# Relative bias of the attention scores: an identity matmul on TensorE in place of an addition on VectorE

## The reference

```python
def diff_attention(q, k, v, rel_bias, lam):
    for i in range(S // Q_BLOCK):
        q0 = i * Q_BLOCK
        end = q0 + Q_BLOCK
        s = jnp.einsum('bqhmd,bkhmd->bhmqk', q[:, q0:end], k[:, :end]).astype(jnp.float32) * scale
        rel = jnp.arange(q0, end)[:, None] - jnp.arange(end)[None, :]
        bias = jnp.transpose(bias_tab[t5_bucket(rel)], (2, 0, 1))
        s = s + bias[None, :, None]
        s = jnp.where(rel >= 0, s, -jnp.inf)
        p = jax.nn.softmax(s, axis=-1)
        a = p[:, :, 0] - lam * p[:, :, 1]
        outs.append(jnp.einsum('bhqk,bkhv->bqhv', a.astype(v.dtype), v[:, :end]))
```

## Time and profile before

| | |
|---|---|
| median of three executions | 2799.29 us |
| profiled execution, its own time | 2801.21 us |
| its span in the trace | 2799.4 us |
| TensorE busy | 2624.7 us, 94% |
| VectorE busy | 1155.1 us, 41% |
| ScalarE busy | 831.7 us, 30% |
| mean granted TensorE clock | 0.969 |

### The profile page before, as it was taken

How to read it: one execution, slowest core, us unless ns; L and a number is a source line. 1 busy time by engine, 2 the same in 40 slices (tenths; PEclk the granted TensorE clock), 3 DMA queues, 4 the chain that set the end, 5 groups by cost and what they waited for, 6 DMA issues and landing times. The chain is left out here.

```text
span 2799.4 us, 30661 instructions
## 1 busy us (share of the span) xinstructions
PE 2624.7 (94%) x12450; PEld 2124.2 (76%) x12450; DVE 1155.1 (41%) x1839; ACT 831.7 (30%) x1463; POOL 140.8 (5%) x165
## 2 busy tenths in 40 slices
PE   8699989879999999999999998996999999999997
PEld 7588866658788888878777886764878888887876
DVE  0556355645333321135662455555531111113554
ACT  0422244434211111134553124444421111113343
POOL 0001100002000000001010010000200000000000
PEclk9999989989999999999999998997999999999999
DMA  5262010012444411144451111001221111114544
GB/s 199 77 207 86 24 46 23 8 61 91 158 136 135 143 46 53 45 143 164 137 174 57 41 39 38 23 16 46 98 76 45 48 51 46 53 45 138 178 135 151
DMA packets 209080, 243.61 MB, mean 87 GB/s; under 512 B 9531, under 2 KB 170156, under 8 KB 207916
## 3 DMA queue, kind: packets, MB, share of 16 engines
q1 hardware_dynamic: 197644, 200.74, 22.6%
q0 software_dynamic: 11296, 40.92, 4.2%
HBM read 224.05 MB, written 17.58 MB: 86 GB/s over the span
## 5 line engine op out<-in xcount | busy, mean ns | idle before, releaser
L1731 PE MATMUL ps<-hT,wsp 128*128 128x512 f32 (+1 forms) x2080 | 832.5, 400 | 20.2 <-DVE F L1359 10.1
L1733 PE MATMUL ps<-hT,wsp 128*128 128x512 f32 (+1 forms) x2080 | 818.4, 393 | 0.0
L1732 PE MATMUL ps<-hT,wsp 128*128 128x512 f32 (+1 forms) x2080 | 818.0, 393 | 0.0
L1099 DVE TENSOR_TENSOR wsp<-raw,wsp 128x1024 fp32r<-128x1024 f32 (+2 forms) x140 | 168.0, 1200 | 864.1 <-ACT wsp L662 698.6
L1731 PEld LDWEIGHTS ps<-hT,wsp 128*128 128x128 f32 (+1 forms) x2080 | 391.5, 188 | 127.6 <-issue 34.7
L1733 PEld LDWEIGHTS ps<-hT,wsp 128*128 128x128 f32 (+1 forms) x2080 | 391.6, 188 | 88.7 <-issue 1.6
L1732 PEld LDWEIGHTS ps<-hT,wsp 128*128 128x128 f32 (+1 forms) x2080 | 391.7, 188 | 81.9 <-issue 1.1
L662 ACT ACTIVATE wsp<-raw 128x1024 fp32r<-128x1024 f32 x84 | 89.1, 1060 | 778.5 <-PE ps L1733 614.0
L2060 PE MATMUL ps<-wsp,asp 128*128 128x512 f32 x1080 | 255.1, 393 | 3.3 <-DVE asp L1629 3.0
L2060 PE MATMUL ps<-hT,asp 128*128 128x512 f32 x1032 | 247.7, 397 | 10.5 <-DVE asp L1629 10.3
L2060 PEld LDWEIGHTS ps<-wsp,asp 128*128 128x128 f32 x1080 | 202.5, 188 | 49.5 <-issue 4.9
(11 more groups left out here) (193 smaller groups left out, 2518.3 us busy)
## 6 DMA issues: line engine op xcount, KB each, us to landing
raw<-in_w_down SPq DMA_DIRECT2D x104, 512.0 KB, 3.5
raw<-in_w_gate_up SPq DMA_DIRECT2D x88, 512.0 KB, 3.9
F<-in_w_mod SPq DMA_DIRECT2D x80, 512.0 KB, 4.9
raw<-in_w_in SPq DMA_DIRECT2D x48, 512.0 KB, 3.8
out_x<-W POOLq DMA_DIRECT2D x32, 512.0 KB, 3.5
F<-in_w_down SPq DMA_DIRECT2D x28, 512.0 KB, 4.3
W<-out_x POOLq DMA_DIRECT2D x24, 512.0 KB, 5.9
raw<-in_w_out SPq DMA_DIRECT2D x16, 512.0 KB, 3.5
```

The source lines that it names most:

```text
L1099: v.tensor_tensor(wsp[0:np_, r, 1, 0:w], raw[0:np_, r, 0:w], wsp[0:np_, r, 0, 0:w].bitcast(F32), ALU.subtract).then_inc(s_lo, 1)
L1731: mm(o, a(0), b(0), start=start, stop=False)
L1732: mm(o, a(0), b(1), start=False, stop=False)
L1733: return mm(o, a(1), b(0), start=False, stop=stop)
```

## The change

For each score block, TensorE now also multiplies the identity with the bias, into the same PSUM columns, without the start flag, so that it adds to the scores that are there. The addition on VectorE, its semaphore `s_ba` and its wait go. The wait for the loaded bias moves from VectorE to TensorE, before the first scores of each head. `s_qk` is now given by the last identity matmul of each map m. The number of identity matmuls is 2 for each block and 4 for b = 4, whose 256 columns lie across a border of 512.

```diff
@@ -1381,12 +1381,7 @@
                 def maxes(h, b, m):
 
                     at, n = l * 64 + h * 16 + 2 * b + m, (b + 1) * P
-                    w = min(n, NEAR)
                     dve.wait_ge(s_qk, 1 + at + 1)
-                    near = pair(1 + m)[:, n - w:n]
-                    o = h * NEAR + NEAR - w
-                    v.tensor_tensor(near, near, bias[:, o:o + w], ALU.add).then_inc(s_ba, 1)
-                    dve.wait_ge(s_ba, at + 1)
                     v.tensor_reduce(ast[:, A_NM + 2 * b + m:A_NM + 2 * b + m + 1],
                                     pair(1 + m)[:, 0:n], AX.X, ALU.max, negate=True
                                     ).then_inc(s_mx, 1)
@@ -1472,7 +1467,6 @@
-                dve.wait_ge(s_bias, l * 16 + 16)
                 maxes(0, 0, 0)
@@ -1968,6 +1962,7 @@
                     n = (b + 1) * P
                     pe.wait_ge(s_ex, 1 + l * 64 + h * 16 + 2 * b)
                     if b == 0:
+                        pe.wait_ge(s_bias, l * 16 + 16)
                         pe.wait_ge(s_fe, evacuated(l, (7, 8, 11, 14)[h]))
                     for c0 in range(0, n, 512):
                         w = min(512, n - c0)
@@ -1976,9 +1971,15 @@
                             last = mm(pair(1 + m)[:, c0:c0 + w],
                                       F[rows, Fq + h * S + b * P:Fq + h * S + b * P + P],
                                       F[rows, Fk[h % 2] + c0:Fk[h % 2] + c0 + w],
-                                      start=True, stop=True)
-                            if c0 + w == n:
-                                last.then_inc(s_qk, 1)
+                                      start=True, stop=False, skip_group_check=True)
+                    near = min(n, NEAR)
+                    for m in range(2):
+                        for c0 in range((n - near) // 512 * 512, n, 512):
+                            a, z = max(c0, n - near), min(c0 + 512, n)
+                            o = h * NEAR + NEAR - n
+                            last = mm(pair(1 + m)[:, a:z], ident, bias[:, o + a:o + z],
+                                      start=False, stop=True, skip_group_check=True)
+                        last.then_inc(s_qk, 1)
```

More of the change, by code:

```diff
@@ L314, in build @@
         s_fin = sem("s_fin")
-        s_qk, s_ba, s_mx = sem("s_qk"), sem("s_ba"), sem("s_mx")
+        s_qk, s_mx = sem("s_qk"), sem("s_mx")
         s_ex, s_rc, s_co, s_ad = sem("s_ex"), sem("s_rc"), sem("s_co"), sem("s_ad")
```

## The result

The changed kernel takes 2804.99 us (median of 20 executions, 2799.39 to 2811.37), the kernel before in the same measurements 2798.70 us. The ratio is 1.0020, with a 95% interval of 1.0013 to 1.0028: slower by 5.6 us by the ratio and by 6.3 us between the two medians. That is on the side that was forecast and in the range, but only about half of the +11 us. The profiled execution of the changed kernel took 2809.4 us, one of its longer ones.

The account below looks back on a forecast made before the run. TensorE was taken to bound heads 1 and 2, a chain through VectorE and ScalarE head 3. Head 0 +2.3, heads 1 and 2 +7.1, head 3 -3.9 make +5.5 us a layer, +11 in all: 2810 us, range 2797 to 2826.

Parts of the forecast that it names:

- the 0.88 of the sum: TensorE's float32 price for a block's two identity matmuls of 256 columns: 0.88 us, if not hidden in waits.
- the five waits: TensorE's waits over 0.5 us in heads 1 and 2, 5.2 us together, expected to take in added work or shrink.
- The interval of the value copy: Heads 1 and 2: two fewer additions before the copy give -1.8 us, and the clock staying up behind it -1.6.
- the rounds: Head 3, five chain rounds with late additions on VectorE: each 0.92 us shorter, the identity matmuls hidden in front.
- a changed granted clock in head 0 and head 3: Stated sign that the prediction is wrong: granted clock in these heads differing from before.
- The tight block of head 0: Block at 374.81 to 380.93 us: +1.8 us if the clock stays low, -1.6 if up; taken as +0.2.
- The end of head 3: Last chain round of the attention: 0.92 us shorter from the additions, with no clock gain counted.
- rival 1: Clock stays up in heads 0 and 3 because TensorE idles less: -3.9 us a layer, 2791.5 us; chance 0.06 in full.
- Rival 1 in half: Half of the clock falls in heads 0 and 3 avoided: about 2801 us; chance 0.13.
- The eighth block of head 0: Last but one interval worked out for head 0: a 0.82 us wait takes in the 0.88 us, leaving +0.1.
- Rival 2: Whole attention: no wait gives anything back, 19 to 20 us a layer slower, 2839 us; chance 0.09.
- Rival 3: All heads: identity matmuls priced as float32r, 0.23 us a block, -8.3 us a layer, 2783 us; chance 0.04.

Follow-up runs that it names:

- e5: Changed kernel with its identity matmuls issued a second time, discarded, ahead of the scores; 2837.70 us, ratio 1.0143 to the kernel before.
- e12: Repeat run with identity matmuls only in the blocks whose interval got shorter in the changed kernel, VectorE additions elsewhere; 2781.59 us, ratio 0.9934 to before.
- e2: Changed kernel without the identity matmuls, so no bias and no mask is added; 2770.84 us, ratio 0.9902 to the kernel before.
- e7: Changed kernel with identity matmuls in heads 1 and 2 only, VectorE additions in the other heads; 2808.23 us, ratio 1.0036 to before.
- e9: Kernel before plus four discarded identity matmuls a layer in TensorE's last waits of the attention; 2792.94 us, ratio 0.9974 to before.
- e10: Changed kernel with identity and bias rounded to float32r and the identity matmuls in float32r; 2783.61 us, ratio 0.9941 to before.
- e3: Kernel before plus discarded identity matmuls ahead of the scores in nine blocks of heads 0 and 3, VectorE additions kept; 2806.27 us, ratio 1.0020.

## Why the prediction was right in sign and wrong in size

**Right.** The bound of the two parts, and so the sign. In heads 1 and 2 TensorE had no room: most full blocks cost 0.85 to 0.90 us for the 0.88 of the sum (e5 confirms the price by itself), and four of the five waits went. The interval of the value copy got shorter by 2.5 us, as worked out (0.92 us of additions and 1.6 of clock), and the clock behind it stayed up: heads 1 and 2 have 1.00. In head 3 the rounds gained 0.87 to 1.03 us for 0.92. The moved wait for the bias held nothing: no wait of TensorE in the changed kernel's trace ends with it. That 2804.99 us lies above 2804.9, the prediction's own border between same and slower, is luck, as it does so by a tenth of a microsecond.

**The step that failed is the clock.** The prediction had named a changed granted clock in head 0 and head 3 as a sign that it is wrong, and it changed, from 0.85 to 0.93 and from 0.75 to 0.83. The sum counted on a clock that comes back in one place only, behind the value copy. It came back at two more, where one term was mis-sized and the other put at nothing:

- The tight block of head 0 (374.81 to 380.93 us before). I had both ends, +1.8 with a low clock and -1.6 with a high one, and took +0.2. In three of four layers it is 4.66 us, in one 5.95, for 6.16 before: -1.2 us in the mean, 1.4 us from the forecast. These are the rows of layer 0 that answer to the one of 2.50 us in the earlier trace rows, first in the second trace of the changed kernel and then in its first:

```profile
374.10 1.35 PE L1971 MATMUL ps<-F 64*128 64x512 f32 x8 [1.59 <-ACT F L877]
```

```profile
373.08 1.67 PE L1971 MATMUL ps<-F 64*128 64x512 f32 x8 [1.59 <-ACT F L877]
```

  In both the waits of 1.40 and 2.45 us had become 0.49 and 1.59 us. In the second trace the clock did not fall (1.00 from 373 to 377 us). In the first it did (0.62 over the same window), and the interval is the one of 5.95 us. So the shorter waits alone do not settle it, and whether it falls is in part luck: e12 has 4.66 us in one layer and 6.04 in the other, with the same code. In e2, without the identity matmuls, the interval is 5.17 and 5.03 us.
- The end of head 3: -1.6 us in the mean for -0.9. In three of four layers the first transposes behind the chain take 0.66 us in place of 1.11; in the fourth they take 1.11 and the interval is 23.77 us, 0.9 us shorter as forecast. I had counted 0.92 us for the round and nothing for the clock there, though it stood among the prices of rival 1. The row before, in the changed kernel, and in e7, whose head 3 has the old code:

```profile
598.12 1.11 PE L1990 MATMUL ps<-cst,F 128*128 128x128 f32 x4 [1.74 <-DVE F L1409]
```

```profile
600.71 0.66 PE L1991 MATMUL ps<-cst,F 128*128 128x128 f32 x4 [1.74 <-DVE F L1404]
```

```profile
602.14 0.66 PE L2010 MATMUL ps<-cst,F 128*128 128x128 f32 x4 [1.74 <-DVE F L1420]
```

  The wait in front is 1.74 us in all three. The last interval of e7 is 24.08 and 23.52 us, so the clock's 0.7 us here do not need the change in head 3; what brings them is open.

Together 2.1 us a layer. I sized them so because I tied a fall to the one wait in front of it. Rival 1 in half (about 2801 us) had the mechanism, and the result, 2805, lies between it and my value. That work in idle time alone brings the clock back, and that this makes the kernel faster, is shown by e9, not only argued. The section on oscillation of the page "TensorE: Matmul & The Clock Gate" of the Trainium skill, beside which I put that rival, has it that a loop that keeps the array fed stays at full rate. The trace of e9 agrees, with 0.76 and 1.00 in its last two windows where the kernel before has 0.50.

**Smaller terms.** The eighth block of head 0 cost 0.7 us for 0.1. I let its 0.88 us vanish in a wait of 0.82 us for a copy on ScalarE. But that copy stands behind ScalarE's square of the weighted values, which waits for TensorE, so it came later too. The changed kernel's timeline of ScalarE:

```profile
403.05 0.28 ACT L944 ACTIVATE W<-ps 128x128 f32<-128x128 f32 x1 [0.86 <-PE ps L2003]
```

  The wait only shrank to 0.69 us. In heads 1 and 2 the sum was 0.6 us too high, mostly the eighth block of head 1 (-0.8 for -0.5) and the two waits of 0.66 us.

**The other rivals.** Rival 2, that no wait gives anything back: e2 shows 13.3 us a layer given back. Rival 3, the float32r price: the change does not have it, but e10 does, at 0.20 to 0.25 us for most blocks and 2783.6 us where the rival's arithmetic gave 2783. That it meets so closely is in part luck: e10's attention is 6.6 us a layer shorter than before, for the 8.3 of the arithmetic, and heads 1 and 2 gave 1.3 us of the 2.6.

**Left open.** Why the stretch between the attentions varies by over 3 us between two traces of one kernel and by 7 us over all runs, and whether its mean depends on the kernel; what decides between the two outcomes of the tight block and of the last interval; and why the changed kernel's times spread over 12 us where those of before mostly lie within 4. This spread goes with the clock: its four executions under 2801 us have a mean granted clock of 0.980 to 0.982, its four over 2808 us one of 0.975 to 0.977.

## What to carry to other kernels

An addition moved from VectorE to an idle-looking TensorE is priced block by block, not by the busy share: here it lost 0.87 us in each block where TensorE was fed and won 0.9 us in each block of a chain, and using it only in the second kind turned +6 us into -17. Look at the number format before the place, if the operand may be rounded as this bias was: float32r cost a quarter of float32 with two matmuls of 256 columns, and half with four of 128. And where an engine with a throttled clock idles in a chain, write down for every low-clock stretch what the change does to the idle time before it.

## What the runs showed of the hardware

Work that nobody needs made the kernel faster: four discarded matmuls a layer, 5 to 7 us in all, of which the trace shows 4.5 where they stand, by bringing the granted clock from 1.2 back to 2.4 GHz some 7 us sooner. Ahead of the scores, in nine blocks a layer, discarded matmuls cost 6 us (e3). Adding to PSUM by an identity matmul between matmuls on 64 rows and others on 128 cost most full blocks 0.85 to 0.90 us in float32 (the changed kernel) and 0.20 to 0.25 us in float32r (e10). For two matmuls of 256 columns that is no more than the 0.88 and 0.23 us that the rows of matmuls without such a switch give. And on the same code the length of the 1085 us between the two attentions went from 1086.3 to 1089.5 us with the clock lost in it, which is half of what this change did to the kernel.
